# Forming the weight sums of three down projections by accumulating transfers in device memory instead of on VectorE

## The chip, the cores and the metric

The kernel runs on one core of a Trainium2 chip. The metric is the device time of one execution in microseconds (us); lower is better. The kernel before takes 1844.03 us, the median of three runs (1843.58 to 1845.5). Engines are named as in the profile: PE is TensorE's matmul, PEld its weight load, DVE is VectorE, ACT is ScalarE, POOL is GpSimd, SP is SyncE, which here only issues transfers.

## The reference

One sequence of 512 tokens of width 1024 goes through a first block (depth 1) and a second block (depth 2). Each of the three layers ends in a feed-forward part whose last matmul is the down projection; these are what the change is about:

```
# first block                                # second block, for l in 0, 1
a  = square(relu(h2 @ w_up))                 z  = dwconv(h2 @ w_up[l]); zg, zv = split(z)
ff = a @ w_down        # (512,4096)(4096,1024)  x = x + (silu(zg) * zv) @ w_down[l]  # (512,2816)(2816,1024)
```

Ahead of them stand pooling and stick-breaking attention (first block), and latent attention with a 31-tap depthwise convolution (each layer of the second). All is in float32.

## The kernel before

All large matmuls are done as three float32r matmuls (high times high, low times high, high times low). So each weight chunk (128 by 512, 256 KB) is loaded by SP into a raw slot, rounded by ACT to its high part (`w_hi`), and DVE takes the rest (`w_lo`, counted by the semaphore `w_split`). PE then uses it and counts `w_used`.

The three down projections are multiplied in Winograd's form of a 2 by 2 block product, with seven products in place of eight. For that, each pair q of inner blocks (16 pairs in the first block, 11 in each layer of the second; 38 in all) has its four weight blocks w11, w12, w21, w22 combined into four sums t1 to t4. In the kernel before these sums are made ahead of time, while the layer's earlier weights are still being multiplied:

- SP loads the four blocks of a pair into four buffers in on-chip memory (L889 for the first block, L996 for the second).
- DVE makes the four sums in place, one instruction each, in `factor_sum`, and counts each in `t_made`. They are strewn among DVE's other work by the tables `FIRST_SUMS` and `SUM_ORDER`.
- SP stores the four sums to a tensor in device memory, `factor_sums1` or `factor_sums` (L895, L1003).

In the down projection (L920 for the first block, L1026 for the second) SP loads the chunks in the order `DOWN_ORDER`: first the products with w11, t3, t2, t1 of all pairs (`PASS1`), then those with w21, t4, w22 (`PASS2`). A sum is thus read back from device memory like any other weight. Before chunk 4 of a down projection SP waits until the last stores have landed.

Each engine runs its own program in order. POOL's program is short: constants, the windowed sums of the pooling (`pool_group`, L1110 to L1120), then in each layer of the second block the diagonal matrices for the convolution (`diagonals`, L1145) and a sum of squares (L1077). PE's convolution matmuls (L3571) read those diagonals.

## Time and profile before

| | |
|---|---|
| median of 3 runs | 1844.03 us |
| the profiled execution's own time | 1845.35 us |
| its span (first to last instruction) | 1843.5 us |
| mean granted TensorE clock | 0.998 of full |
| PE / PEld / DVE / ACT / POOL busy | 99% / 80% / 77% / 55% / 4% |
| moved by DMA | 281.24 MB, 153 GB/s on the mean |

The profile page gives busy time per engine. Matmuls overlap in the pipeline: a 512-column matmul is shown as 0.39 us long, but one starts each 0.227 us. So PE's busy share says only that it hardly idles. Idle time is shown in front of the instruction that ends it, with the engine or transfer that it waited for.

### The profile page before, as it was taken

The numbers are of one execution on the slowest core, as the hardware profiler recorded it, in microseconds if no ns is written. First come the engines' busy times: TensorE is split into PE (matmuls) and PEld (weight loads), VectorE is DVE, ScalarE is ACT, GpSimd is POOL, SyncE is SP. The second block draws the span as 40 slices with busy tenths as digits, with TensorE's granted clock in tenths as the row PEclk, the third lists the DMA queues.
The fourth block names the chain that finished last, engine by engine and source line by source line (L and its number), as shares of the span: only waits on it lengthen the run. The fifth ranks groups of instructions, "written<-read, shape, count | busy, mean of one in ns | idle before, by whom it ended". The sixth has DMA issues, their size and how long they took to land.

```text
span 1843.5 us, 26684 instructions
## 1 busy us (share of the span) xinstructions
PE 1816.2 (99%) x9225; PEld 1482.6 (80%) x9225; DVE 1416.6 (77%) x2566; ACT 1021.9 (55%) x1911; POOL 75.2 (4%) x110
## 2 busy tenths in 40 slices
PE   8999999999999999999999999999999999999998
PEld 7888878788788878577888888998757878888786
DVE  5887776876687877786578888986877578778978
ACT  6777664544476664566444435664556553344666
POOL 1111100000000000100200000000010020000000
PEclk9999999999999999999999999999999999999999
DMA  4222236398766624511446756643541235676664
GB/s 149 78 78 72 80 123 209 111 318 299 246 220 186 195 78 107 106 46 36 118 154 209 235 190 211 212 156 87 120 84 41 68 108 190 195 246 201 207 195 137
DMA packets 229459, 281.24 MB, mean 153 GB/s; under 512 B 55250, under 2 KB 130016, under 8 KB 229344
## 3 DMA queue, kind: packets, MB, share of 16 engines
q1 hardware_dynamic: 229240, 279.76, 48.7%
q8 instruction: 62, 1.02, 0.2%
q14 instruction: 53, 0.43, 0.1%
q10 hardware_dynamic: 104, 0.03, 0.0%
HBM read 228.98 MB, written 41.94 MB: 147 GB/s over the span
## 4 chain that ended last, share of the span: by engine, by line
PE 87%; DVE 8%; ACT 3%; issue 1%; DMA 1%; SPq 0%; ACTq 0%; DVEq 0%
PE bank_b L3064 14%; PE bank_b L3066 14%; PE bank_b L3065 14%; PE bank_a L3064 11%; PE bank_a L3066 11%; PE bank_a L3065 11%; PE bank_b L3571 2%; PE bank_b L3675 2%; DVE w_lo L1920 2%; DVE arena L1920 1%; PE bank_a L3656 1%; DVE arena L1923 1%; PE bank_a L3091 1%; PE bank_a L3094 1%; PE bank_a L3097 1%
## 5 line engine op out<-in xcount | busy, mean ns | idle before, releaser
L1920 DVE TENSOR_TENSOR w_lo<-w_raw,w_hi 128x512 fp32r<-128x512 f32 (+1 forms) x599 | 391.9, 672 | 198.5 <-ACT w_hi L1577 127.9
L3064 PE MATMUL bank_b<-h_hi,w_hi 128*128 128x512 f32 (+1 forms) x952 | 372.9, 392 | 1.0 <-DVE w_lo L1920 0.6
L3066 PE MATMUL bank_b<-h_hi,w_lo 128*128 128x512 f32 (+1 forms) x952 | 369.3, 388 | 0.0
L3065 PE MATMUL bank_b<-h_lo,w_hi 128*128 128x512 f32 (+1 forms) x952 | 369.0, 388 | 0.0
L1577 ACT ACTIVATE w_hi<-w_raw 128x512 fp32r<-128x512 f32 (+3 forms) x308 | 176.4, 589 | 244.7 <-PE bank_b L3066 93.4
L3064 PEld LDWEIGHTS bank_b<-h_hi,w_hi 128*128 128x128 f32 x952 | 178.8, 188 | 41.1 <-DVE w_lo L1920 2.9
L3065 PEld LDWEIGHTS bank_b<-h_lo,w_hi 128*128 128x128 f32 x952 | 178.8, 188 | 36.9 <-issue 1.4
L3066 PEld LDWEIGHTS bank_b<-h_hi,w_lo 128*128 128x128 f32 x952 | 178.7, 188 | 36.9
L3064 PE MATMUL bank_a<-h_hi,w_hi 128*128 128x512 f32 x513 | 201.1, 392 | 0.4
L3066 PE MATMUL bank_a<-h_hi,w_lo 128*128 128x512 f32 x513 | 199.6, 389 | 0.0
L3065 PE MATMUL bank_a<-h_lo,w_hi 128*128 128x512 f32 x513 | 199.6, 389 | 0.0
L1166 ACT ACTIVATE w_hi<-w_raw 128x512 fp32r<-128x512 f32 x161 | 97.3, 625 | 114.3 <-PE bank_b L3066 55.3
L1920 DVE TENSOR_TENSOR split<-arena,split 128x512 fp32r<-128x512 f32 (+4 forms) x220 | 123.0, 581 | 40.0 <-ACT split L1512 22.6
L1923 DVE SCALAR_TENSOR_TENSOR arena<-arena,cols_all 128x512 f32<-128x512 f32 x176 | 126.3, 745 | 0.0
L3064 PEld LDWEIGHTS bank_a<-h_hi,w_hi 128*128 128x128 f32 x513 | 96.3, 188 | 23.4 <-DVE w_lo L1920 3.3
L3066 PEld LDWEIGHTS bank_a<-h_hi,w_lo 128*128 128x128 f32 x513 | 96.3, 188 | 20.2
L3065 PEld LDWEIGHTS bank_a<-h_lo,w_hi 128*128 128x128 f32 x513 | 96.3, 188 | 20.1 <-issue 0.5
L1501 ACT ACTIVATE w_hi<-w_raw 128x512 fp32r<-128x512 f32 x130 | 78.3, 625 | 42.0 <-PE bank_b L3066 31.1
L1512 ACT ACTIVATE split<-arena 128x512 fp32r<-128x512 f32 (+1 forms) x114 | 62.5, 554 | 46.7 <-PE bank_b L3066 27.7
L1920 DVE TENSOR_TENSOR split_f<-split_f 128x512 f32<-128x512 f32 x102 | 69.7, 685 | 8.1 <-DMA split_f<-in_w_down_dram 8.0
L1823 ACT ACTIVATE arena<-arena,cols_all 128x512 f32<-128x512 f32 x80 | 58.8, 806 | 30.3 <-DVE arena L1920 30.3
L3064 PE MATMUL bank_b<-split,w_hi 128*128 128x512 f32 (+1 forms) x196 | 72.7, 371 | 0.0
(456 smaller groups left out, 3554.1 us busy)
## 6 DMA issues: line engine op xcount, KB each, us to landing
w_raw<-in_w_up_dram SPq DMA_DIRECT2D x240, 256.0 KB, 4.0
split_f<-in_w_down_dram SPq DMA_DIRECT2D x110, 256.0 KB, 4.7
factor_sums<-split_f SPq DMA_DIRECT2D x104, 256.0 KB, 4.2
w_raw<-factor_sums SPq DMA_DIRECT2D x79, 256.0 KB, 3.5
w_raw<-in_w_down_dram SPq DMA_DIRECT2D x51, 256.0 KB, 3.0
ssum<-in_w_down_dram SPq DMA_DIRECT2D x34, 256.0 KB, 3.1
arena<-arena SPq DMA_DIRECT2D x32, 268.0 KB, 4.1
w_raw<-in_w_in_dram SPq DMA_DIRECT2D x64, 128.0 KB, 2.4
```

The lines of the kernel that those rows point to most:

```text
L1166: nc.scalar.activation(w_hi[:, s, :], w_raw[:, s, :], ACT.Copy).then_inc(w_round, 1)
L1501: nc.scalar.activation(ring_hi(l, n), raw_of(l, n), ACT.Copy).then_inc(w_round, 1)
L1512: nc.scalar.activation(as_hi[:, u % 4, 0:unit_cols(l, u)], unit(l, u), ACT.Copy).then_inc(as_round, 1)
L1577: nc.scalar.activation(w_hi[:, s, 0:c], w_raw[:, s, 0:c], ACT.Copy).then_inc(w_round, 1)
L1823: nc.scalar.activation(cz[:, j, :], zp[:, j, 1:1 + S], ACT.Identity, scale=cols_all[:, l, bass.ds(tile + (L_FTAP + 2 * F2T), 1)], bias=col ...
L1920: return nc.vector.tensor_tensor(out_, a, b, op)
L1923: return nc.vector.scalar_tensor_tensor(out=out_, in0=a, scalar=s, in1=b, op0=op0, op1=op1)
L3064: nc.tensor.matmul(out_, a_hi, b_hi, start=start, stop=False, skip_group_check=loose)
L3065: nc.tensor.matmul(out_, a_hi, b_lo, start=False, stop=False, skip_group_check=loose)
L3066: return nc.tensor.matmul(out_, a_lo, b_hi, start=False, stop=stop, skip_group_check=loose)
L3571: last = nc.tensor.matmul(conv_banks[j][rows, :], diag[:, r, rows], stacks[j % 2][:, c, SHIFTS * r:SHIFTS * r + S], start=r == 0, stop=r = ...
L3675: last = nc.tensor.matmul(bank_b[rows, i % 2, c], vv[:, kb, i, rows], pts[(2 * j + hd) % len(pts)][:, kb * P:kb * P + P], start=kb == 0, s ...
```

## The change

DVE's `factor_sum`, its buffers and SP's loads and stores for it are gone. After `pool_group(3)` POOL issues transfers from device memory to device memory: plain copies of the blocks into the tensors of sums, and then transfers that add their source onto the destination (`accum_op`). As only additions are used, the definitions of the sums change sign here and there, and the sums of activations and the final updates on DVE take the opposite sign in exchange (the same number of instructions, `ALU.add` and `ALU.subtract` swapped). `move` issues one transfer, `moved` lets POOL wait until all so far have landed, and `t_made` now counts landed transfers. SP waits for `t_made` before each load of a sum in the down projection. The number of transfers that carry the sums is the same (304 of 256 KB).

```diff
+MOVES_FIRST, MOVES_LAST, MOVES = 6, 2, 8
...
+        def sums_made(l, kind, q):
+
+            if l >= 0:
+                return 16 * (MOVES * DPS[FIRST] + MOVES * (l * DP + q + 1))
+            if kind == "t4":
+                return 16 * (MOVES_FIRST * DPS[FIRST] + 4 * MOVES_LAST * (q // 4 + 1))
+            return 16 * MOVES_FIRST * (q + 1)
...
-            def first_moves(n):
-
-                for q in FIRST_STORES.get(n, ()):
-                    store_first(q)
-                for q, part in FIRST_LOADS.get(n, ()):
-                    sem, landed = sums_moved(FIRST, q, 0)
-                    sp_.wait_ge(sem, landed)
-                    sp_.dma_start(sum_buf(FIRST, q)[part], down_v[:, 2 * q + part // 2, part % 2, :]).then_inc(sem, 16)
-
-            def store_first(q):
-
-                sp_.wait_ge(t_made, 4 * q + 4)
-                for n, kind in enumerate(("t2", "t1", "t4", "t3")):
-                    sp_.dma_start(factor_sums1[q, KINDS.index(kind)], sum_buf(FIRST, q)[n]).then_inc(sums_moved(FIRST, q, 0)[0], 16)
-
...
-                if n == SLOTS:
-                    for m in range(N_DOWN, N_DOWN + SLOTS + 4):
-                        first_moves(m)
-                    store_first(DPS[FIRST] - 1)
-                    for m in range(DPS[FIRST] - FIRST_BUFS, DPS[FIRST]):
-                        sp_.wait_ge(*sums_moved(FIRST, m, 2))
                 if n < SLOTS:
                     sp_.wait_ge(w_split, N_DOWN + n - SLOTS + 1)
                 elif n >= RING:
                     sp_.wait_ge(w_split, N_DOWN + n - RING + 1)
                 if kind in KINDS:
+                    sp_.wait_ge(t_made, sums_made(FIRST, kind, q))
                     src = factor_sums1[q, KINDS.index(kind)]
...
+            moves = 0
+
+            def move(into, src, op=None):
+
+                nonlocal moves
+                moves += 1
+                if op is None:
+                    pool.dma_start(into, src).then_inc(t_made, 16)
+                else:
+                    pool.dma_start(into, src, accum_op=op, max_dma_last_dim=4 * S).then_inc(t_made, 16)
+
+            def moved():
+
+                pool.wait_ge(t_made, 16 * moves)
+
+            def blocks(src, q):
+
+                return [[src[:, 2 * q + two, half, :] for half in range(2)] for two in range(2)]
+
+            for q in range(DPS[FIRST]):
+                (w11, w12), (w21, w22) = blocks(down_v, q)
+                t1, t2, t3, t4 = (factor_sums1[q, n] for n in range(4))
+                move(t1, w11)
+                move(t3, w22)
+                move(t2, w11)
+                moved()
+                move(t1, w12, ALU.add)
+                move(t3, w12, ALU.add)
+                moved()
+                move(t2, t3, ALU.add)
+                moved()
+            for q0 in range(0, DPS[FIRST], 4):
+                for q in range(q0, q0 + 4):
+                    move(factor_sums1[q, 3], blocks(down_v, q)[1][0])
+                moved()
+                for q in range(q0, q0 + 4):
+                    move(factor_sums1[q, 3], factor_sums1[q, 1], ALU.add)
+                moved()
+
+            def layer_sums(l, pairs):
+
+                for q in pairs:
+                    (w11, w12), (w21, w22) = blocks(down2_v[l], q)
+                    t1, t2, t3, t4 = (factor_sums[l, q, n] for n in range(4))
+                    move(t1, w11)
+                    move(t3, w22)
+                    move(t2, w11)
+                    move(t4, w21)
+                    moved()
+                    move(t1, w12, ALU.add)
+                    move(t3, w12, ALU.add)
+                    moved()
+                    move(t2, t3, ALU.add)
+                    moved()
+                    move(t4, t2, ALU.add)
+                    moved()
+
             for l in range(DEPTH2):
+                if l == 0:
+                    layer_sums(0, range(5))
                 was = before(l)
                 sq0, added0 = was["sq_ready"], was["sq_added"]
                 pool.wait_ge(sq_added, added0 + KT - 1)
...
+                if l == 0:
+                    layer_sums(0, range(5, DP))
+                    layer_sums(1, range(DP))
...
-            for q in (DPS[FIRST] - 3, DPS[FIRST] - 2):
-                act.wait_ge(*sums_moved(FIRST, q, 2))
...
-            def factor_sum(l, q, turn):
-
-                w11, w12, w21, w22 = sum_buf(l, q)
-                if turn == 0:
-                    dve.wait_ge(*sums_moved(l, q, 1))
-                else:
-                    dve.wait_ge(t_made, 4 * PAIRS_BEFORE[l] + 4 * q + turn)
-                into, a, b, op = ((w22, w22, w12, ALU.subtract), (w12, w12, w11, ALU.subtract), (w11, w22, w11, ALU.add),
-                                  (w21, w21, w11, ALU.subtract))[turn]
-                tt(into, a, b, op).then_inc(t_made, 1)
 
             def act_sums(l, q, made):
 
                 x11, x21, x22 = arena[:, 2 * q, 0:HS], arena[:, 2 * q, HS:S], arena[:, 2 * q + 1, HS:S]
                 dve.wait_ge(a_ready, made)
-                tt(s13(l, q)[:, 0:HS], x21, x22, ALU.add).then_inc(s_made, 1)
+                tt(s13(l, q)[:, 0:HS], x21, x22, ALU.subtract).then_inc(s_made, 1)
                 tt(s13(l, q)[:, HS:S], x11, x21, ALU.subtract).then_inc(s_made, 1)
...
-                tt(arena[:, 2 * q, 0:HS], arena[:, 2 * q + 1, 0:HS], arena[:, 2 * q, HS:S], ALU.subtract).then_inc(s4_made, 1)
-
...
```

Where the work stands in the engines' programs. POOL of the kernel before, from the end of the last pooling group to its end (L1145 are the diagonals of a layer, L1077 its sum of squares):

```order
L1120 TENSOR_TENSOR arena<-sq,arena 128x496
L1145 TENSOR_TENSOR arena<-cols_all,lanes 128x128 x26
L1077 TENSOR_TENSOR ssum<-sq 128x512
L1077 TENSOR_TENSOR ssum<-ssum,sq 128x512 x6
L1145 TENSOR_TENSOR arena<-cols_all,lanes 128x128 x26
L1077 TENSOR_TENSOR ssum<-sq 128x512
L1077 TENSOR_TENSOR ssum<-ssum,sq 128x512 x6
L348 UNCONDITIONAL_BRANCH
```

POOL of the change around the diagonals of the second block's first layer (its lines are numbered anew: L1057 is a copying transfer, L1059 an adding one, L1122 the diagonals, L995 the sum of squares):

```order
L1057 DMA factor_sums<-in_w_down_dram 128x512 x4
L1059 DMA factor_sums<-in_w_down_dram 128x512 x2
L1059 DMA factor_sums<-factor_sums 128x512 x2
L1122 TENSOR_TENSOR arena<-cols_all,lanes 128x128 x26
L995 TENSOR_TENSOR ssum<-sq 128x512
L995 TENSOR_TENSOR ssum<-ssum,sq 128x512 x6
L1057 DMA factor_sums<-in_w_down_dram 128x512 x4
L1059 DMA factor_sums<-in_w_down_dram 128x512 x2
```

What was one run of tensor instructions now has 168 transfers ahead of the first layer's diagonals (128 for the first block, 40 for 5 pairs of layer 0) and 136 ahead of the second layer's (6 pairs of layer 0, 11 of layer 1), each diagonal behind all of them.

SP of the kernel before, at the start of the first down projection (L920), with the semaphores waited for in brackets:

```order
L920 DMA w_raw<-factor_sums 128x512 [waits w_split]
L895 DMA factor_sums<-split_f 128x512 [waits t_made]
L895 DMA factor_sums<-split_f 128x512 x3
L895 DMA factor_sums<-ssum 128x512 [waits t_made]
L895 DMA factor_sums<-var 128x512
L895 DMA factor_sums<-rs 128x512
L895 DMA factor_sums<-rstd 128x512
L920 DMA ssum<-factor_sums 128x512 [waits raw_moved2,raw_moved1,raw_moved0]
L920 DMA var<-factor_sums 128x512
L920 DMA rs<-factor_sums 128x512
L920 DMA rstd<-factor_sums 128x512
```

SP of the change further on in the same down projection (now L856):

```order
L856 DMA w_raw<-factor_sums 128x512 [waits t_made,w_split]
L856 DMA ssum<-in_w_down_dram 128x512 [waits w_split]
L856 DMA var<-in_w_down_dram 128x512 [waits w_split]
L856 DMA rs<-factor_sums 128x512 [waits t_made,w_split]
L856 DMA rstd<-in_w_down_dram 128x512 [waits w_split]
```

The stores between SP's loads are gone, and the loads of sums wait for POOL's transfers by `t_made`.

## Rows read from the trace of the kernel before

**Rows 1.** The page: busy time, then PE, granted clock and DMA in 40 slices.

```profile
PE 1816.2 (99%) x9225; PEld 1482.6 (80%) x9225; DVE 1416.6 (77%) x2566; ACT 1021.9 (55%) x1911; POOL 75.2 (4%) x110
...
PE   8999999999999999999999999999999999999998
...
PEclk9999999999999999999999999999999999999999
DMA  4222236398766624511446756643541235676664
```

**Rows 2.** Waits of PE: all the run, then of 1700 to 1750 alone (us, times, longest).

```profile
PE bank_a L3171 <- DMA arena<-in_x_dram: 4.6, 1, 4.6
PE bank_a L3064 <- ACT arena L1743: 4.4, 6, 1.3
PE bank_a L3064 <- DVE split L1920: 3.3, 4, 2.2
...
PE bank_b L3064 <- DVE w_lo L1920: 0.6, 3, 0.2
...
PE bank_a L3064 <- DVE split L1920: 0.6, 2, 0.3
```

**Rows 3.** Stretches: length, then busy time (instructions) of each engine, clock, DMA share, GB/s.

```profile
348.00:485.00 137.00, 137.00 (x604) 113.09 (x603) 96.95 (x170) 59.94 (x107) 0.00 (x0) 1.00 0.84 283
912.00:1127.00 215.00, 214.75 (x942) 175.87 (x941) 172.24 (x287) 88.76 (x139) 0.33 (x1) 1.00 0.62 199
1250.00:1338.00 88.00, 87.52 (x381) 71.04 (x380) 63.70 (x116) 41.73 (x75) 3.10 (x6) 1.00 0.43 103
1500.00:1706.00 206.00, 205.85 (x905) 168.69 (x904) 165.32 (x277) 85.54 (x134) 0.00 (x0) 1.00 0.61 199
```

**Rows 4.** One form of DVE's weight sums: busy us, mean ns, then idle before.

```profile
L1920 DVE TENSOR_TENSOR split_f<-split_f 128x512 f32<-128x512 f32 x102 | 69.7, 685 | 8.1 <-DMA split_f<-in_w_down_dram 8.0
```

**Rows 5.** Start of the first down projection, in time: start us, us, instruction; PE, then ACT.

```profile
504.44 0.57 PE L3064 MATMUL bank_a<-w_hi,split 128*128 128x512 f32 x1 [2.20 <-DVE split L1920]
504.81 0.63 PE L3065 MATMUL bank_a<-w_lo,split 128*128 128x512 f32 x1
...
508.16 0.40 PE L3064 MATMUL bank_a<-w_hi,split 128*128 128x512 f32 x1
508.40 0.40 PE L3065 MATMUL bank_a<-w_lo,split 128*128 128x512 f32 x1
...
502.34 0.63 ACT L1501 ACTIVATE w_hi<-w_raw 128x512 fp32r<-128x512 f32 x1 [2.09 <-PE bank_b L3066]
502.87 0.61 ACT L1512 ACTIVATE split<-arena 128x512 fp32r<-128x512 f32 x1
```

**Rows 6.** POOL in time, from its last pooling instruction; idle before in brackets.

```profile
202.47 1.25 POOL L1120 TENSOR_TENSOR arena<-sq,arena 128x496 f32<-128x496 f32 x1 [4.01 <-DVE w_lo L1920]
685.30 3.04 POOL L1145 TENSOR_TENSOR arena<-cols_all,lanes 128x128 f32<-128x128 f32 x6 [481.57 <-DVE ssum L1920]
...
906.15 6.17 POOL L1077 TENSOR_TENSOR ssum<-ssum,sq 128x512 f32<-128x512 f32 x4 [3.77 <-ACT sq L1180]
1266.24 3.10 POOL L1145 TENSOR_TENSOR arena<-cols_all,lanes 128x128 f32<-128x128 f32 x6 [353.91 <-DVE ssum L1920]
```

**Rows 7.** PE's first convolution matmuls of either layer, in time.

```profile
754.92 5.36 PE L3571 MATMUL bank_a<-arena 128*32 128x512 f32 x48
1338.65 2.35 PE L3571 MATMUL bank_a<-arena 128*32 128x512 f32 x20
```

**Rows 8.** SP's loads in time: t3 of pair 0, t3 of pair 15, t4 of pairs 0 and 1; layer 0.

```profile
488.76 0.33 SPq L920 DMA_DIRECT2D w_raw<-factor_sums  x1
570.37 0.32 SPq L920 DMA_DIRECT2D var<-factor_sums  x1
577.15 1.69 SPq L920 DMA_DIRECT2D w_raw<-factor_sums  x2
1132.24 0.43 SPq L1026 DMA_DIRECT2D var<-factor_sums  x1
```

**Rows 9.** Transfers of `split_f`: issue time in ns (min/median/max), then issue to landing in us.

```profile
L895 SPq DMA_DIRECT2D factor_sums<-split_f x48: 429/462/1111, 299.2 to 495.3; - x48
DMA to landing us min/median/max: 2.5/4.4/7.3
```

**Rows 10.** Transfers of `factor_sums` (stores and loads back): issue to landing in us.

```profile
DMA to landing us min/median/max: 2.0/3.8/6.4
```

More of the change, by code:

```diff
@@ L16 @@
 from contextlib import ExitStack
-from itertools import islice
 import concourse.bass as bass
@@ L509, in two_blocks @@
         first_raw = (ssum[:, :], var[:, :], arena[:, 31, :], split_f[:, 20, :])
-        sum_bufs = [[split_f[:, n, :] for n in range(4)], [split_f[:, n, :] for n in range(4, 8)], [sq[:, n, :] for n in range(4)],
-                    [split_f[:, 8, :], split_f[:, 9, :], rs0[:, :], rs1[:, :]]]
         factor_sums = nc.dram_tensor("factor_sums", (DEPTH2, DP, 4, P, S), F32)
@@ L519, in two_blocks @@
         raw1 = (ssum[:, :], var[:, :], rs1[:, :], rstd[:, 0, :])
-        bufs1 = [[split_f[:, n, :] for n in range(4)], [split_f[:, n, :] for n in range(4, 8)], list(raw1)]
-        early1 = [split_f[:, n, :] for n in range(17, 21)]
         factor_sums1 = nc.dram_tensor("factor_sums1", (F1T // 2, 4, P, S), F32)
@@ L1022, in _ @@
                     if kind in KINDS:
+                        sp_.wait_ge(t_made, sums_made(l, kind, q))
                         src = factor_sums[l, q, KINDS.index(kind)]
@@ L1974, in fourth_sum, with update @@
                 dve.wait_ge(as_ready, units_before(l) + 2 * q + 1)
-                tt(arena[:, 2 * q, 0:HS], arena[:, 2 * q + 1, 0:HS], arena[:, 2 * q, HS:S], ALU.subtract).then_inc(s4_made, 1)
-            def update(name, t, after, into, src, made, count):
+                tt(arena[:, 2 * q, 0:HS], arena[:, 2 * q + 1, 0:HS], arena[:, 2 * q, HS:S], ALU.add).then_inc(s4_made, 1)
+            def update(name, t, after, into, src, made, count, op=ALU.add):
                 dve.wait_ge(made, count)
@@ L2934, in ffn_tiles @@
                                 ALU.mult, ALU.add).then_inc(done, 1)
-                            for q, turn in islice(sums, 1):
-                                factor_sum(l, q, turn)
                         split(tap // 2)
```

84 lines of the change are left out of this document (13 added, 71 removed).

## The prediction

> **What bounds the kernel now.** I read the page's busy times first. PE is busy 1816.2 of 1843.5 us and no other engine is near it: DVE has 77%, POOL 4% [rows 1]. The 40 slices show the same from end to end, at full clock. As busy matmuls overlap, I then asked the waits of PE, for only what PE waits for can be won by unburdening another engine. PE waits for DVE 3.3 us for its splits and 0.6 us for `w_lo`, in all [rows 2]. Then the stretches in which DVE makes the weight sums: 348 to 485 (first block) and 912 to 1127 and 1500 to 1706 (second). PE has 604, 942 and 905 matmuls in 137, 215 and 206 us, one each 0.227 to 0.228 us, and idles for 0.00, 0.25 and 0.15 us. In 1250 to 1338, where DVE makes no weight sums, the pace is 381 in 88 us, 0.231 us each, no faster [rows 3]. So the sums lie wholly beside the matmuls, and they don't slow their pace either.
>
> **What is removed.** 38 pairs by 4 sums are 152 DVE instructions (102 of them in the form of [rows 4]) by 0.685 us, 104 us of DVE's 1416.6. All of it lies beside a PE that hardly idles, so I cost it at nothing but the waits. Of PE's 3.3 us for DVE's splits, 2.2 us is one gap at 502.2 to 504.4, the start of the first down projection [rows 5], and 0.6 us lies at 1700 to 1750, the start of the last one [rows 2].
>
> The change takes ACT's wait for the stores of pairs 13 and 14 out of just this place, so it has to be asked whether the 2.2 us goes. ACT rounds four weight chunks and then the units of the activations. The fourth chunk is rounded at 502.34, after a wait of 2.09 us that ended with a PE matmul (its slot had to come free), and the first unit follows at 502.87, at once [rows 5]. So the removed wait was over, and what is late is PE's own last matmul of the up projection followed by ACT, DVE and PE in turn. ACT's order is the same in the change: the gap stays. The slow stretch behind it stays too: nine matmuls start 0.43 us apart instead of 0.23, which is 1.8 us (the first starts at 504.44, the tenth at 508.16, so 3.72 us for nine). SP's loads of the down projection no longer wait behind eight stores, but PE has no wait for a transfer there [rows 2], so that is worth nothing. The gain I take is 0.5 us, most of the 0.6 us at 1700 to 1750.
>
> **What is added.** 304 transfers on POOL, each 256 KB, device memory to device memory, in waves: POOL issues a few, waits until all have landed, issues the next. The chain is serial, and what stands behind it in POOL's order is waited for by PE. The trace has no transfer issued by POOL, none from device memory to device memory and none that adds. So I set up the deadlines exactly and bound the price.
>
> Deadlines. POOL is free at 202.47 + 1.25 = 203.7 and after that does nothing until the diagonals at 685.3 [rows 6]. But these 685.3 are no deadline: PE first reads diagonals at 754.9 [rows 7]. By then POOL has to make 76 waves (first block 16 x 3 and 4 x 2, layer 0 5 x 4), 551 us for them. Within these, t1 to t3 of pair 15 are wanted at 570.4 and t4 of pairs 0 to 3 at 577.2 [rows 8]. After the sum of squares at 906.15 + 6.17 = 912.3 [rows 6], POOL has 17 pairs of 4 waves ahead of the second layer's diagonals, which PE reads at 1338.65 [rows 7]: 426.3 us, 25.1 us a pair, 6.3 us a wave. That is the tightest. Layer 0's own down projection begins at 1132 [rows 8], by when its 6 pairs are long made, if a pair takes under 36 us.
>
> Price. Let s be the time to issue one more transfer, c the time from issue to landing of a copy, a that of an adding one. The nearest rows are SP's transfers of the same size to and from `split_f` under the same load: s = 0.46 us, c = 4.4 us median, with 2.5 and 7.3 us as the ends [rows 9]. `factor_sums` alone lands in 2.0 to 6.4 us, median 3.8 [rows 10]. Low end: 2.0 us for either kind. High end, if read and write came strictly one after the other: c = 3.8 + 3.9, say 7.7, and a = 11.6 with the second operand's read. I take c = 4.4, since reading and writing stream through together, and for a the middle between the median and the longest landing, 5.9 us (an estimate from 4.4 and 7.3), as an add reads twice what it writes. With s = 0.45:
> - a pair of the first block, t1 to t3: (2s + c) + (s + a) + a = 17.6 us; 16 pairs end at 203.7 + 281 = 485, and 570 is wanted.
> - four t4: (3s + c) + (3s + a) = 13.0 us; the first four end at 498 (577 wanted), all at 537.
> - a pair of the second block: (3s + c) + (s + a) + a + a = 23.9 us; 5 pairs end at 656, before POOL's old 685.
> - 17 pairs: 406 us, from 912 to 1319, where 1338.65 is wanted. It fits with 20 us to spare, or 0.4 us in a.
>
> The diagonals begin some 50 us later than now in the second layer (1319 for 1266), which their cover, PE's work until 1338, hides. Waits added on SP: each load of a sum waits for `t_made`, and all later weight loads are behind it; they are satisfied before SP comes there in all three projections. Traffic: the sums' transfers keep their number, but device memory now sees 304 writes where it saw 152, and 456 reads where it saw 152 (a copy reads once, each of the 152 adds twice), 40 and 80 MB more, spread over 204 to 1320. In 348 to 485 DMA is at 0.84 busy today without one wait of PE [rows 3], so I cost the spreading at nothing.
>
> A rule speaks against my price of the add. The Trainium skill, Collectives: The Full Stack, section on the bandwidth ceiling, says that a reduce runs at half the rate of a copy because its two source reads share one ring. Taken on the whole landing time, that makes a = 8.8 us, the second rival below. Taken on the moving part alone it is little. No row here shows it.
>
> **Sum.** 1843.5 - 0.5 + 0 = 1843.0 us of span, with the 1.85 us outside it 1844.85 for a profiled execution that took 1845.35. That execution lies 1.3 us above the median of the runs, so the median comes to 1843.5 us.
>
> **Rivals.**
> - Faster: 1840. Freed of 104 us, DVE and ACT meet PE in time at 502, and the 2.2 us gap and the 1.8 us of slow matmuls behind it go. Against it: ACT there waited for PE, not for DVE [rows 5].
> - Small loss, 1848 to 1855. More read and write traffic in stretches where SP's loads are urgent, or POOL's issuing work slowing DVE, makes PE wait now and then; ten waits of 0.5 to 1 us would do. Against it: the 0.84 busy stretch.
> - Slower, the chain misses its last deadline. The mechanism: POOL reaches the second layer's diagonals late, and PE stands at its first convolution matmul. It decides from a = 6.3 us on, and then costs 51 us for each us in a. With a = 7.3, the longest landing in [rows 9], a pair takes 28.1 us, 17 take 478, and PE waits 51 us: 1895. The first chain, 524 us, ends at 727 and still fits.
> - Far slower, a = 8.8: a pair 32.6 us, 17 take 554, 128 us late; the first chain 23.4 x 16 + 15.9 x 4 + 32.6 x 5 = 601 us, 49 us late at 754.9 (7 of them already at pair 15). Together 177: 2021. At the high end, a pair of 44.3 us makes 327 us late, and the first chain 274: 2445.
>
> The Trainium skill, DMA: Bandwidth & Descriptors, section on the anatomy of one DMA issued by GpSimd, gives 2.0 us plus bytes over 436 GB/s, 2.6 us here as an estimate; by that alone a pair would take some 12 us and no deadline would be near. The loads and stores of the trace take 3.8 to 4.4 us on the median, so the rows decide.
>
> **How the numbers follow.** A measurement of this kernel tells from no change what is over about 0.2%, 3.7 us. Chances: no change as forecast 0.48 (1841 to 1847); faster 0.10; small loss 0.10; the last deadline missed 0.20 (1855 to 1935); far slower 0.12. So slower has 0.42. The range takes in faster, the small loss and the greater part of the missed deadline: 1840 to 1910. Its upper end leaves out about 0.18.
>
> **What would show it.** Right: DVE's busy time down by about 104 us with PE's matmul count and pace unchanged; the wait of 2.2 us at 502 still there; POOL's diagonals of the second layer starting between 1290 and 1338; no wait of PE for L1145's successor, L1122. A landing time of the adding transfers of 5.9 us confirms the price, below 6.3 the verdict. Wrong: PE idle before the convolution matmuls with POOL named as the releaser; SP waiting for `t_made` in the first down projection, which would show that 22.9 us a pair is passed; or the gap at 502 gone.

## The result and the profile after

The change made the kernel slower by 0.6%: 1856.95 us, the median of six runs (1851.69 to 1857.69), for 1845.36 of six runs of the kernel before beside them (1843.58 to 1847.42). The medians differ by 11.6 us; the ratio is 1.0059 [1.0049, 1.0069], which is 9 to 13 us. The forecast was no change. The profiled execution took 1856.91 us, its span is 1854.8 us, and 11.3 us more than the span before is what has to be explained.

The page of the changed kernel, the lines that answer to [rows 1], and of its DMA and chain sections the lines needed below (q0 is the queue of POOL's transfers: packets, MB, share of the time of the 16 DMA engines):

```profile
PE 1816.5 (98%) x9225; PEld 1484.2 (80%) x9225; DVE 1329.3 (72%) x2414; ACT 1022.9 (55%) x1911; POOL 281.3 (15%) x414
...
POOL 1111222222222211100222211112220020000000
...
DMA  4222577677799966411477778887841123333554
...
q0 software_dynamic: 34048, 79.71, 21.3%
...
HBM read 268.83 MB, written 81.79 MB: 189 GB/s over the span
...
PE 68%; DMA 20%; DVE 4%; issue 3%; POOL 2%; ACT 2%; SPq 0%; DVEq 0%; ACTq 0%; POOLq 0%
```

PE does the same 9225 matmuls in the same busy time. DVE is relieved of 152 instructions and 87 us of busy time (1416.6 to 1329.3). The 104 us forecast were 152 by 0.685, and the durations of DVE's instructions do add up to 104 us less (1464.7 for 1569.1); busy time counts a stretch in which two overlap only once, so it falls by 0.57 us for each. The chain that ended last now runs to 20% through DMA and to 2% through POOL: the chain of waves of transfers has become a part of the critical path.

What PE waits for, in all, as in [rows 2] (us, times, longest):

```profile
PE bank_a L3534 <- POOL arena L1122: 5.3, 1, 5.3
...
PE bank_b L3027 <- issue: 4.0, 2, 3.9
PE bank_a L3027 <- DVE split L1898: 2.8, 2, 2.2
PE bank_a L3066 <- DVE ssum L1898: 2.6, 2, 2.1
```

Of the last one the kernel before has this:

```profile
PE bank_a L3103 <- DVE ssum L1920: 1.0, 2, 0.5
```

Two waits are new, and the last has grown: its longer one, now 2.1 us for 0.5, ends at 1313.3. The first is the one that the prediction named as the sign of a missed deadline: a convolution matmul with POOL's diagonals (L1122) as the releaser. PE in time at the four places in question (start us, us, instruction, idle before), for [rows 5] and [rows 7]:

```profile
504.56 0.47 PE L3027 MATMUL bank_a<-w_hi,split 128*128 128x512 f32 x1 [2.20 <-DVE split L1898]
...
753.51 5.36 PE L3534 MATMUL bank_a<-arena 128*32 128x512 f32 x48
...
1336.03 0.47 PE L3027 MATMUL bank_b<-split,w_hi 128*128 128x512 f32 x1 [3.86 <-issue]
...
1349.59 7.49 PE L3534 MATMUL bank_a<-arena 128*32 128x512 f32 x48 [5.31 <-POOL arena L1122]
```

The gap at 502 is there unchanged with its 2.20 us, and the first layer's convolution starts at 753.5, 1.4 us earlier than before. The second layer's starts at 1349.6, where it was 1338.65: 10.9 us of the 11.3 have arisen by then.

POOL in time, for [rows 6]: the first layer's diagonals, then the first pair of the second chain (L1057 a plain copy, L1059 an adding transfer), then its end.

```profile
711.64 2.64 POOL L1122 TENSOR_TENSOR arena<-cols_all,lanes 128x128 f32<-128x128 f32 x6 [3.40 <-DMA factor_sums<-factor_sums]
...
911.01 2.14 POOL L1057 DMA_DIRECT2D factor_sums<-in_w_down_dram  x4
920.59 1.72 POOL L1059 DMA_DIRECT2D factor_sums<-in_w_down_dram  x2 [7.44 <-DMA factor_sums<-in_w_down_dram]
928.21 0.80 POOL L1059 DMA_DIRECT2D factor_sums<-factor_sums  x1 [5.89 <-DMA factor_sums<-in_w_down_dram]
932.50 0.81 POOL L1059 DMA_DIRECT2D factor_sums<-factor_sums  x1 [3.49 <-DMA factor_sums<-factor_sums]
936.97 2.12 POOL L1057 DMA_DIRECT2D factor_sums<-in_w_down_dram  x4 [3.65 <-DMA factor_sums<-factor_sums]
...
1344.97 0.81 POOL L1059 DMA_DIRECT2D factor_sums<-factor_sums  x1 [3.51 <-DMA factor_sums<-factor_sums]
1349.05 3.54 POOL L1122 TENSOR_TENSOR arena<-cols_all,lanes 128x128 f32<-128x128 f32 x7 [3.28 <-DMA factor_sums<-factor_sums]
```

The first pair's waves take 9.58, 7.62, 4.29 and 4.47 us, 25.96 in all. The 17 pairs run from 911.0 to 1349.05, 438 us, 25.8 us a pair on the mean, where 25.1 was the break-even and 23.9 the forecast. They are not alike: from start to start the first eight (911 to 1105) take 24.3 us each, the next five (to 1252) 29.4, the last four 24.3. PE's matmul starts 0.54 us after the diagonals begin.

How long POOL takes to issue a transfer, and how long one takes to land, for [rows 9] and [rows 10] (ns min/median/max, first and last start; then us):

```profile
L1057 POOL DMA_DIRECT2D factor_sums<-in_w_down_dram x152: 523/552/771, 204.2 to 1327.3; - x152
...
DMA to landing us min/median/max: 2.7/4.7/8.2
```

```profile
L1059 POOL DMA_DIRECT2D factor_sums<-in_w_down_dram x76: 839/871/1172, 209.8 to 1334.5; - x76
L1059 POOL DMA_DIRECT2D factor_sums<-factor_sums x76: 802/807/1771, 217.3 to 1345.0; - x76
...
DMA to landing us min/median/max: 3.9/5.2/11.4
```

The other new wait, 3.9 us before 1336.03, does not name POOL. The profile has only "issue" for it, so the link is read from the times: PE starts 0.1 us after ACT's three squares out of `bank_b` (L1160, 1334.38 to 1335.93), the bank that PE writes next. In ACT's order they stand behind the rounding of a small weight chunk, and that waited for its load. Here ACT at this chunk in the change (the first fence) and in the kernel before (the second):

```profile
1334.06 0.42 ACT L1555 ACTIVATE w_hi<-w_raw 128x256 fp32r<-128x256 f32 x1 [5.44 <-DMA w_raw<-in_w_uq_dram]
```

```profile
1329.69 0.42 ACT L1577 ACTIVATE w_hi<-w_raw 128x256 fp32r<-128x256 f32 x1 [0.87 <-DMA w_raw<-in_w_uq_dram]
```

ACT gets that chunk 4.4 us later, while POOL's last waves are under way. SP did not issue its loads later: they start at 1324.0 here and at 1324.2 before. They land later. Issue to landing (us, min/median/max) of the ten loads of `w_uq` issued up to 1330.3, in the change and in the kernel before:

```profile
DMA to landing us min/median/max: 3.7/4.4/6.4
```

```profile
DMA to landing us min/median/max: 1.7/1.9/3.9
```

The stretches around it (length, busy time of each engine, granted clock, DMA share, GB/s), the first two as in [rows 3]:

```profile
348.00:485.00 137.00, 137.00 (x605) 113.06 (x604) 68.89 (x122) 59.73 (x107) 31.61 (x47) 1.00 0.74 187
912.00:1127.00 215.00, 214.78 (x944) 176.74 (x944) 149.76 (x248) 91.02 (x142) 47.20 (x70) 1.00 0.77 188
1100.00:1250.00 150.00, 150.00 (x1105) 142.99 (x1104) 124.96 (x216) 93.85 (x167) 28.01 (x41) 1.00 0.84 232
...
1336.00:1340.00 4.00, 3.97 (x9) 2.55 (x10) 2.98 (x7) 2.29 (x5) 0.00 (x0) 0.61 1.07 168
1348.00:1352.00 4.00, 2.41 (x12) 0.68 (x16) 2.78 (x5) 3.91 (x9) 2.95 (x6) 0.50 0.11 22
```

Behind each of the two idle times the granted clock is lower: 0.50 in 1348 to 1352, which is the lower level of 1.2 GHz, and 0.61 on the mean in 1336 to 1340, where nine matmuls fill 4 us. The wait of 2.1 us before 1313.3, the idle time of 3.9 us and the slow stretch behind it make PE ready for the convolution only at 1344.3 (1349.59 less 5.31). Counted from the start of layer 0's down projection, PE gets there 7.5 us sooner where nothing disturbs it (198.05 us in the table below, for 205.6 here). That by itself is not paid for: the diagonals came at 1349.05 anyway. So POOL's lateness alone suffices for the 11 us, and what the late loads would cost without it is for an experiment.

### The profile page after: what moved, and what is told of

The parts are those of the page before. It is cut to its first block, busy times and chain, and to the rows that moved or that the text cites. A ratio compares the mean times of both kernels' runs of the same rounds, so it can differ in the third digit from the quotient of the medians.

```text
span 1854.8 us, 26670 instructions
## 1 busy us (share of the span) xinstructions
PE 1816.5 (98%) x9225; PEld 1484.2 (80%) x9225; DVE 1329.3 (72%) x2414; ACT 1022.9 (55%) x1911; POOL 281.3 (15%) x414
## 3 DMA queue, kind: packets, MB, share of 16 engines
q0 software_dynamic: 34048, 79.71, 21.3%
HBM read 268.83 MB, written 81.79 MB: 189 GB/s over the span
## 4 chain that ended last, share of the span: by engine, by line
PE 68%; DMA 20%; DVE 4%; issue 3%; POOL 2%; ACT 2%; SPq 0%; DVEq 0%; ACTq 0%; POOLq 0%
PE bank_b L3027 11%; DMA factor_sums<-in_w_down_dram 11%; PE bank_b L3029 11%; PE bank_b L3028 11%; DMA factor_sums<-factor_sums 9%; PE bank_a L3027 8%; PE bank_a L3029 8%; PE bank_a L3028 8%; PE bank_b L3534 2%; PE bank_b L3638 2%; POOL factor_sums L1057 1%; PE bank_a L3619 1%; DVE w_lo L1898 1%; PE bank_a L3054 1%; PE bank_a L3057 1%
## 5 line engine op out<-in xcount | busy, mean ns | idle before, releaser
L1901 DVE SCALAR_TENSOR_TENSOR arena<-arena,cols_all 128x512 f32<-128x512 f32 x176 | 120.5, 744 | 0.0
L1059 POOL DMA_DIRECT2D factor_sums<-factor_sums x76 | 61.9, 911 | 330.2 <-DMA factor_sums<-in_w_down_dram 230.7
L1057 POOL DMA_DIRECT2D factor_sums<-in_w_down_dram x152 | 81.2, 544 | 194.5 <-DMA factor_sums<-factor_sums 183.2
L1059 POOL DMA_DIRECT2D factor_sums<-in_w_down_dram x76 | 64.7, 998 | 206.6 <-DMA factor_sums<-in_w_down_dram 202.5
```

Of the source, the lines that this page charges most:

```text
L1057: pool.dma_start(into, src).then_inc(t_made, 16)
L1059: pool.dma_start(into, src, accum_op=op, max_dma_last_dim=4 * S).then_inc(t_made, 16)
L1901: return nc.vector.scalar_tensor_tensor(out=out_, in0=a, scalar=s, in1=b, op0=op0, op1=op1)
```

## Experiments

The theory after the result: the second chain ends some 11 us too late, because a pair costs 25.8 us on the mean. Its rivals: that the transfers beside the small loads cost the time by themselves, and that the end of the chain is of no matter. Whether DVE's relief is worth nothing was open too. Kernels that were timed stood beside 15 to 31 runs of the kernel before, with medians of 1844.42 to 1845.13 us.

**One pair more ahead of the first layer's diagonals, one fewer behind.**

```diff
-                    layer_sums(0, range(5))
+                    layer_sums(0, range(6))
...
-                    layer_sums(0, range(5, DP))
+                    layer_sums(0, range(6, DP))
```

> The change, with six pairs of layer 0 summed ahead of that layer's diagonals in place of five, so that 16 pairs in place of 17 stand ahead of the second layer's diagonals. Theory (the loss is POOL's lateness at the second layer's diagonals): at 25.8 us a pair the second chain ends near 1323, before PE's first convolution matmul at 1338, the first chain ends near 736 and PE wants its diagonals at 754, so nothing is late: 1844 to 1846 us, 11 to 12 below the change. Rival (the loss is spread, from the larger traffic and POOL's issuing): at most one third of it goes, 1852 or more.

Measured: 1846.4 us (1844.67 to 1850.05, 11 runs), ratio 1.0015 [1.0006, 1.0024]. POOL at the second layer's diagonals, then PE at the convolution:

```profile
1318.70 3.40 POOL L1122 TENSOR_TENSOR arena<-cols_all,lanes 128x128 f32<-128x128 f32 x6 [3.60 <-DMA factor_sums<-factor_sums]
```

```profile
1340.31 5.36 PE L3534 MATMUL bank_a<-arena 128*32 128x512 f32 x48
```

The diagonals of the chain of 16 pairs start 21.6 us before PE wants them, and PE does not wait. A change that only moves one pair takes back 10.6 us. It doesn't tell the two theories apart, though: with one pair fewer the chain also ends before the small loads of 1324 to 1340. And 1.3 us are left between the medians (1 to 4 by the interval). In the trace the wait for `ssum`, here before 1315.2, is 1.6 us for 0.5, beside the chain's last waves.

**Six pairs of layer 1 only after that layer's sum of squares.** They are not needed before its own down projection.

```diff
-                    layer_sums(1, range(DP))
+                    layer_sums(1, range(5))
+                else:
+                    layer_sums(1, range(5, DP))
```

> The change, with pairs 5 to 10 of layer 1 summed after that layer's sum of squares (from about 1490 on), so that 11 pairs stand ahead of the second layer's diagonals and the chain ends near 1195. Theory: 1844 to 1846 us, the same as with six pairs, though the transfers are now away from the whole stretch 1195 to 1490. Rival (traffic beside the second layer's small weight loads also costs where nothing is late): this kernel is faster than the one with six pairs by 2 us or more. The late pairs end near 1650, and the down projection wants pair 5 after 1715.

Measured: 1844.95 us (1843.39 to 1847.52, 11 runs), ratio 1.0005 [0.9996, 1.0014], no difference from before. POOL reaches the diagonals about when the kernel before did (1266.24), and the wait for `ssum` is back at 0.5 us:

```profile
1268.26 1.96 POOL L1122 TENSOR_TENSOR arena<-cols_all,lanes 128x128 f32<-128x128 f32 x3 [74.70 <-DVE ssum L1900]
```

**Transfers beside the small loads, with the chain in time.** The kernel with six pairs, and after its diagonals six spare transfers of the same sizes and kinds into a tensor that nobody reads.

```diff
...
                 diagonals(0)
+                if l == 1:
+                    (w11, w12), (w21, w22) = blocks(down2_v[l], 0)
+                    for n, src in enumerate((w11, w22, w11, w21)):
+                        move(spare[n], src)
+                    moved()
+                    for n in range(2):
+                        move(spare[n], w12, ALU.add)
+                    moved()
...
```

> As the kernel with six pairs, and after the first seven diagonals of the second layer POOL moves six transfers (four copies, two adding) into a tensor that nobody reads, from about 1323 to 1340, beside the small weight loads of that layer. If contention alone makes those loads late, PE idles near 1332 for about 4 us, as it did with the change, and the time is 4 to 6 us above that with six pairs. If only lateness counts, it is the same as with six pairs within 1 us.

Measured: 1850.03 us (1848.31 to 1851.02, 9 runs), ratio 1.0028 [1.0018, 1.0038]; 3.6 us more than with six pairs alone, near the 4 to 6 us expected of contention. POOL at the spare transfers, and PE at its one long wait before the convolution:

```profile
1320.69 4.29 POOL L1123 TENSOR_TENSOR arena<-cols_all,lanes 128x128 f32<-128x128 f32 x6 [3.78 <-DMA factor_sums<-factor_sums]
1324.93 2.15 POOL L1058 DMA_DIRECT2D spare<-in_w_down_dram  x4
```

```profile
1316.45 2.07 PE L3075 MATMUL bank_a<-ssum,ones 128*128 128x512 f32 x2 [3.70 <-DVE ssum L1907]
```

But this wait ends 8.5 us before the first spare transfer is issued. It is the wait for `ssum` again (1.6 us with six pairs), beside the last waves of the chain itself, with the clock at 0.50 in 1316 to 1320 behind it. PE has lost nothing more when it comes to the convolution: in the table below it is there 4.9 us later than with six pairs, all of it by 1326.4, and behind it up to the next up projection 0.4 us are added. So the spare transfers did not cost this execution its time, and what makes the medians differ by 3.6 us is open. (The spare tensor also stands ahead of `factor_sums` in device memory; whether that matters wasn't tried.)

That transfers in flight hold up the small loads is shown by comparing the traces. The wait for `ssum` near 1313 is 0.5 us in the kernel before, in the one with sums of one column below, and in all six versions whose transfers are over by then. It is 1.6, 2.1, 2.5 and 3.7 us in the four where the chain still runs: six pairs, the change, four pairs, and this one. The small loads of 1324 to 1330 land after 4.4 us on the median beside the change's last waves, after 2.0 us with six pairs. In these executions such waits, with the slow clock behind them, make PE 1.1 us (six pairs), 6.0 us (this one) and 7.5 us (the change) later at the convolution than PE is undisturbed; in the change that lay inside POOL's lateness. The proof that lateness by itself costs time is the next experiment.

**One more pair behind than in the change.** Four pairs of layer 0 ahead of its diagonals, 18 behind; the diff is that of the first experiment with 4 for 6.

> The change with four pairs of layer 0 ahead of the first layer's diagonals and 18 pairs ahead of the second's. By lateness alone each pair more costs its whole 25.8 us: 1878 to 1884 us, with PE waiting some 31 us for L1122 near 1344. If the loss came from traffic or from the number of transfers, which are the same, the time stays at 1857.

Measured: 1878.55 us (1871.84 to 1880.68, 4 runs), ratio 1.019 [1.0174, 1.0206], 21.6 us above the change on the median. Number and kind of the transfers are those of the change. In the profiled execution, at 1871.84 the fastest of the four, PE stands at the convolution (31 us were expected):

```profile
1364.79 1.94 PE L3534 MATMUL bank_a<-arena 128*32 128x512 f32 x8 [23.11 <-POOL arena L1122]
```

**Seven pairs ahead of the first layer's diagonals.** This pushes the first chain to its own deadline.

> The change with seven pairs of layer 0 ahead of the first layer's diagonals. The second chain (15 pairs) ends near 1300, in time; the first ends near 761, 7 to 8 us after PE wants its diagonals at 753.5. Theory of deadlines: PE waits for L1122 near 754 to 761 and no longer at 1344, and the time is 7 to 9 us above that with six pairs, 1853 to 1856. Rival (the loss sits in the second layer's stretch alone, not at whichever deadline is missed): 1844 to 1847.

Measured: 1850.99 us (1848.24 to 1856.11, 4 runs), ratio 1.0044 [1.0027, 1.0062], less than expected. POOL and PE of the profiled execution (1848.66 us):

```profile
758.47 2.16 POOL L1122 TENSOR_TENSOR arena<-cols_all,lanes 128x128 f32<-128x128 f32 x3 [3.35 <-DMA factor_sums<-factor_sums]
```

```profile
751.75 0.47 PE L3027 MATMUL bank_b<-split,w_hi 128*128 128x512 f32 x1 [2.81 <-issue]
...
759.93 5.36 PE L3534 MATMUL bank_a<-arena 128*32 128x512 f32 x48
```

Here the diagonals came 1.5 us before their matmul, and the wait that was expected is not there: PE had already lost its time at 751.75 and at 730.1, where its wait for `ssum` is 2.35 us for 0.5. These are the same two kinds of wait as at 1313 and 1336 in the change, again beside the chain's waves. PE would not have fared better without them, since the diagonals at 758.47 are later than the 754.9 of before. So with 5 pairs the second deadline is missed, with 7 the first, and of the splits tried only 6 fits both.

**The same chain without adding.** Every adding transfer is a plain copy; the sums are not made.

```diff
-                    pool.dma_start(into, src, accum_op=op, max_dma_last_dim=4 * S).then_inc(t_made, 16)
+                    pool.dma_start(into, src).then_inc(t_made, 16)
```

> The change with each adding transfer made a plain copy (the sums are left out: the tensors hold single blocks). Number, order and size are the same. If adding costs only in POOL's issue (0.87 us against 0.55), a pair takes 24.5 us; if it also costs in the engines, since an add reads two operands, a pair takes 20 to 22 us, and the second chain ends at 1250 to 1285 in place of 1349.

One run, 1843.32 us. Issue times, POOL's queue on the page, and the second layer's diagonals:

```profile
L1059 POOL DMA_DIRECT2D factor_sums<-in_w_down_dram x76: 523/523/535, 210.8 to 1258.9; - x76
L1059 POOL DMA_DIRECT2D factor_sums<-factor_sums x76: 486/497/502, 215.2 to 1266.5; - x76
```

```profile
q0 software_dynamic: 20672, 79.71, 13.7%
```

```profile
1270.30 2.65 POOL L1122 TENSOR_TENSOR arena<-cols_all,lanes 128x128 f32<-128x128 f32 x6 [3.32 <-DMA factor_sums<-factor_sums]
```

The chain is 78.8 us shorter (1270.30 for 1349.05), 4.6 us a pair or 1.16 us for each of the 68 waves, of which 51 add. A pair takes 21.1 us on the mean, in the range expected if an add also costs in the engines. From start to start of the waves between 911 and 1100 (means over 7 to 18 waves):

| wave of | copies (this kernel) | as in the change |
|---|---|---|
| 1 transfer | 3.34 us | add: 4.66 us |
| 2 transfers | 5.27 us | adds: 6.83 us |
| 4 copies | 7.83 us | 7.96 us |

An add costs some 1.3 us more than a copy in a wave of one, 1.6 us in a wave of two. Of that 0.3 us is POOL's issuing (0.81 for 0.50 us). The DMA engines have more to do as well: for the same 79.71 MB the packets of POOL's queue take 21.3% of the engines' time with adds and 13.7% without. If the 152 copies cost half of 13.7% in either kernel, an add takes some 2.1 times the engine time of a copy (an estimate), though its wave lasts only 1.4 times as long. The bytes read from device memory don't tell the two apart: the page has 268.83 MB read for both kernels.

**Two pairs a wave.** The transfers of pairs 2n and 2n+1 are issued together, so that there are half as many waits.

```diff
-                for q in pairs:
...
+                for n in range(0, len(pairs), 2):
+                    two = [(blocks(down2_v[l], q), [factor_sums[l, q, m] for m in range(4)]) for q in pairs[n:n + 2]]
+                    for ((w11, w12), (w21, w22)), (t1, t2, t3, t4) in two:
+                        move(t1, w11)
+                        move(t3, w22)
+                        move(t2, w11)
+                        move(t4, w21)
+                    moved()
...
```

> The change with two pairs in each wave in place of one (t4 of the first block stays by fours), the order else the same. If a wave's price is mostly the wait for landing, a group of two pairs takes some 29 to 33 us in place of 51.6: the first chain ends near 600, the second near 1200, nothing is late, and the time is 1843 to 1847. If the price is bytes through the DMA engines, two pairs take 45 us or more and the second chain ends after 1290. Denser bursts could cost PE more beside its loads: above 1847.

Measured: 1843.73 us (1842.56 to 1844.88, 11 runs), ratio 0.9996 [0.9987, 1.0005]. POOL in one group of two pairs, and at the diagonals:

```profile
946.72 4.18 POOL L1058 DMA_DIRECT2D factor_sums<-in_w_down_dram  x8 [5.82 <-DMA factor_sums<-factor_sums]
958.00 3.36 POOL L1060 DMA_DIRECT2D factor_sums<-in_w_down_dram  x4 [7.10 <-DMA factor_sums<-in_w_down_dram]
968.74 1.64 POOL L1060 DMA_DIRECT2D factor_sums<-factor_sums  x2 [7.37 <-DMA factor_sums<-in_w_down_dram]
974.49 1.64 POOL L1060 DMA_DIRECT2D factor_sums<-factor_sums  x2 [4.11 <-DMA factor_sums<-factor_sums]
980.15 4.18 POOL L1058 DMA_DIRECT2D factor_sums<-in_w_down_dram  x8 [4.02 <-DMA factor_sums<-factor_sums]
...
1265.51 3.04 POOL L1128 TENSOR_TENSOR arena<-cols_all,lanes 128x128 f32<-128x128 f32 x6 [26.13 <-DVE ssum L1904]
```

Two pairs take 33.4 us here (946.72 to 980.15), the shortest of eight such groups; they take 33.4 to 44.0, on the mean 37.9 us or 18.9 a pair, more than the 29 to 33 expected and less than the 45 of the rival. The chain is done 26 us before DVE releases the diagonals, and the loss is gone.

**The kernel before, with DVE's weight sums cut to one column.** The instructions and all waits stay; the sums are not made.

```diff
-                tt(into, a, b, op).then_inc(t_made, 1)
+                tt(into[:, 0:1], a[:, 0:1], b[:, 0:1], op).then_inc(t_made, 1)
```

> The kernel before, its 152 weight sums on DVE cut to one column each (so the sums are left out but for a column), everything else in place. DVE has some 95 us less to do. Theory (these sums lie wholly beside the matmuls): 1844 to 1846 us, no difference. Rival (DVE's load does hold PE back somewhere): faster by 3 us or more.

Measured: 1842.19 us (1841.16 to 1842.74, 11 runs), ratio 0.9986 [0.9977, 0.9995], 2.9 us less. That is a small gain whose interval leaves out no change: DVE's sums did cost something. The stretch behind the gap at 502, in the kernel before and in this one:

```profile
500.00:512.00 12.00, 9.80 (x36) 7.66 (x36) 6.60 (x11) 9.91 (x20) 0.00 (x0) 0.86 0.84 271
```

```profile
500.00:512.00 12.00, 9.80 (x43) 7.80 (x42) 6.29 (x10) 9.20 (x18) 0.00 (x0) 1.00 0.75 255
```

Without the fall of the clock to 0.86, seven more matmuls start in these 12 us. But the profiled execution of the change also has full clock there, and others have not, with the same gap of 2.2 us before it, so I can't tie it to the edit.

**Transfers put where loads are light.** Two versions. The first keeps single pairs: 5, 4 and 2 pairs of layer 0, 7 and 4 of layer 1, the middle groups ahead of the sums of squares:

```diff
+                if l == 0:
+                    layer_sums(0, range(5, 9))
+                else:
+                    layer_sums(1, range(7, DP))
                 pool.wait_ge(stat_ready, was["stat_ready"] + 4)
                 add_squares(KT,
...
```

> The change, its transfers placed where PE's weight loads are light: 5 pairs of layer 0 ahead of the diagonals as in the change, 4 pairs of layer 0 after the diagonals (from 782, done near 885), 2 pairs of layer 0 and 7 of layer 1 after the sum of squares (911 to some 1140), the last 4 of layer 1 after its diagonals (1366 to some 1470). Nothing is late by the measured 25.8 us a pair. Theory (lateness plus what the transfers' traffic takes beside the loads): 1843 to 1845, at or a little below the kernel with the late pairs after the sum of squares (1844.95). Rival (placement does not matter once nothing is late): equal to that kernel within 0.5 us.

Measured: 1844.08 us (1842.25 to 1844.83, 11 runs), ratio 0.9996 [0.9987, 1.0005].

The second takes two pairs a wave as above, all 11 pairs of layer 0 ahead of its diagonals, and of layer 1 six pairs ahead of layer 0's sum of squares and five ahead of its own, so that no transfer of POOL lies beside an up projection of the second block:

```diff
-                    layer_sums(0, range(5))
+                    layer_sums(0, range(DP))
...
+                layer_sums(1, range(6, DP) if l else range(6))
                 pool.wait_ge(stat_ready, was["stat_ready"] + 4)
...
```

> Two pairs in each wave, and all transfers kept out of the two stretches in which PE works through the up projections of the second block: all 11 pairs of layer 0 ahead of its diagonals (done near 711, wanted at 753.5), 6 pairs of layer 1 after layer 0's diagonals (782 to 887, the sum of squares is at 897), the last 5 after layer 1's diagonals (1366 to 1471, then the sum of squares at 1481). Theory (what DVE's freedom brings, 2.9 us by the kernel with thin sums, is taken back by transfers beside the up projections): 1841.5 to 1843, below the kernel before by 2 to 3 us and below the one with two pairs a wave by 1. Rival (the take-back is elsewhere): 1843.5 to 1844.5, as with two pairs a wave.

Measured: 1844.64 us (1843.5 to 1849.16, 11 runs), ratio 1.0004 [0.9995, 1.0013]. The expected gain did not come.

**Where the last microseconds are.** Distances between PE's first matmuls of successive parts, from the traces of the profiled executions (us):

| kernel | first down projection to first convolution | to layer 0's up projection | to its down projection | to second convolution | to layer 1's up projection | to its down projection | to the end |
|---|---|---|---|---|---|---|---|
| before | 250.48 | 165.64 | 219.82 | 198.27 | 165.33 | 219.95 | 110.78 |
| sums of one column | 248.88 | 165.54 | 218.95 | 198.05 | 165.52 | 218.93 | 109.95 |
| the change | 248.95 | 165.81 | 219.40 | 210.87 | 167.5 | 218.93 | 109.95 |
| six pairs | 249.67 | 165.82 | 220.23 | 199.15 | 166.02 | 218.93 | 109.95 |
| six pairs and spare transfers | 250.13 | 165.77 | 219.60 | 204.08 | 166.40 | 218.97 | 109.95 |
| late pairs | 250.69 | 165.82 | 219.99 | 198.05 | 165.74 | 220.60 | 109.95 |
| two pairs a wave | 248.99 | 165.46 | 219.91 | 198.03 | 165.74 | 218.98 | 109.94 |
| no transfer beside up projections | 250.78 | 165.85 | 218.98 | 198.05 | 165.82 | 218.93 | 109.95 |

The change against the kernel before, from left to right: -1.5, +0.2, -0.4, +12.6, +2.2, -1.0, -0.8, in sum +11.3. The +2.2 stand behind the wait for POOL, where the clock is at 0.50. The first column goes by the clock at 502: the traces with 250.5 to 250.8 us have 0.86 in 500 to 512, the others 1.00. DVE's relief gives 0.8 us in the last down projection in every version. In an up projection it gives about 1.0 us (218.9 for 219.9), unless POOL's transfers lie beside it: these take between 0.5 and 1.7 us of it back. These are profiles of one execution each, and I show their agreement, not an interval. The last version wins both up projections and has the fall of the clock at 502, which makes its first column 1.9 us longer than with sums of one column; why it came here is open.

## Why the prediction was wrong

**The deadlines were right.** POOL's start at 203.7, the two deadlines at 754.9 and 1338.65 and their order of tightness hold: the chain misses the second only, and where it is given one pair fewer it fits (six pairs), one more and it is 15 to 22 us later (four pairs). The mechanism of the loss is that of the third rival, with its price at the mild end: that rival decided from a pair of 25.1 us on, and a pair took 25.8. Its condition in a, 6.3 us or more, was not met on the mean: a single add took 4.66 us up to 1100, less than my 5.9, and 6.06 between 1100 and 1250. My sign that a landing below 6.3 us confirms the verdict was no sign: the median is 5.2, and the deadline was missed.

**The step that failed is the price of a wave: 23.9 us a pair for all 17, wherever they stand.** Together they cost 438 us for 406, which takes the 20 us to spare and 11 more. By stretches the miss is not spread evenly. The twelve pairs outside 1105 to 1252 cost 24.3 us each, 4 us too much in all; at that price 17 pairs end at 1323 and fit. The five pairs inside cost 29.4 each, 27 us too much. There I costed the waves beside layer 0's down projection like all others. In 1100 to 1250 the DMA engines are busy to 0.84 with 232 GB/s, where the kernel before moved 188 GB/s. In the kernel without adds the five pairs of this stretch are slower too, 24.3 us for 19.7 before it. That the fuller engines are the cause fits all this; no experiment isolates it.

**Within the price, s and a were both wrong.** I took s = 0.45 us, SP's issue time, as the cost of each further transfer in a wave, and a landing time for a single one. Four copies were (3s + c) = 5.75 us by that. Measured are 7.96 us, and the series in the kernel without adds, 3.34, 5.27 and 7.83 us for 1, 2 and 4 copies, shows how: a lone copy is cheaper than I took c for (3.34, issue included, for 4.4), but each further one adds 1.3 to 1.9 us. With eight in a wave it is 12.66 us, 1.2 us each. POOL's issue time of 0.55 us is less than half of that. That the transfers of one wave share what moves them would explain the rest; it is not shown. For adds the same: 4.66 us alone, where I had taken 5.9, and 2.2 us for the second.

By terms a pair in the stretch 911 to 1100 costs 7.96 + 6.83 + 2 x 4.66 = 24.1 us, for 23.9 forecast: the errors of the two terms nearly cancel, by luck. Between 1100 and 1250 it is 8.33 + 8.23 + 2 x 6.06 = 28.7, each kind of wave dearer.

**The margin was misread.** I wrote "20 us to spare, or 0.4 us in a". Spread over 68 waves, 20 us are 0.3 us a wave, less than the difference between any two rows that I had taken my prices from ([rows 9], [rows 10]). A forecast with ends of 2.0 and 7.7 us and a break-even so close to the value taken had no ground for 0.48 on the one side.

**First chain.** Forecast to end at 656, it ended at 711.6. The pairs of the first block took 18.2 us for 17.6, 10 us in all; four t4 took 21.4 us for 13.0, 33 us in all; five pairs 26.1 for 23.9, 11 us. The waves with most transfers are the most underpriced, here by the term s. It was hidden by the 43 us of slack that were left.

**DVE's sums at nothing.** Wrong in size: with the sums cut to one column the kernel takes 2.9 us less (1 to 4 by the interval of its ratio), where I had 0.5. In the profiles 2.7 us of it lie in the second block's two up projections and the last down projection. The first block's up projection gains nothing (147.4 us from 357.0 to 504.4, and the same with sums of one column), and 1.6 us of the profiled execution's gain is the clock at 502. PE's pace of 0.227 to 0.228 us a matmul in [rows 3] looked full, but 1 us in 220 is four matmuls of over 900. The list of waits does not show it either. From start to start, some half of it are single delays (a matmul at 1066.6 starts 0.48 us after the one before it, for 0.23), the rest delays of hundredths of a us in some twenty matmuls.

**The gap at 502** stays with 2.20 us, as argued from ACT's wait for PE. The 1.8 us of slow matmuls behind it, which I said would stay too, are a matter of the clock's fall and come and go between executions.

**Traffic at nothing.** Wrong where small loads are urgent: PE's wait for `ssum` near 1313 grows from 0.5 to between 1.6 and 3.7 us, and in the change another of 3.9 us comes at 1336. The 0.84 busy stretch, from which I argued, had no such loads in it. The bytes were wrong too: I forecast 80 MB more read, counting two reads for an add, and the page has 39.85 MB more, just as much as with plain copies.

**The rules.** A single add took 4.66 us and a single copy 3.34 us from wave to wave, so doubling the whole landing (8.8 us) is not borne out. The rule of the Trainium skill, Collectives: The Full Stack, section on the bandwidth ceiling, is that two source reads on one ring halve the rate; the trace agrees with it for the DMA engines' time alone (2.1 times, by the estimate above). The estimate of 2.6 us from the Trainium skill, DMA: Bandwidth & Descriptors, section on the anatomy of one DMA, lies below the 2.7 us that was the shortest landing and far below the median of 4.7.

## What to carry to other kernels

When work goes to a serial chain of waves with a deadline, measure or bound the wave, not the transfer: what a further transfer in a wave costs (here 1.2 to 2.2 us for 256 KB) is not its issue time, and waves beside heavy loads cost a fifth more (29.4 us a pair for 24.3). Price each stretch of the chain by what runs beside it. Compare the slack per wave with the spread of the durations that the price was taken from; if it is smaller, the forecast is open, whatever the middle says. If the chain is too long, merge waves of independent items (25.8 to 18.9 us a pair here) or move one item past the deadline before doubting the idea; but with the engine that was relieved off the critical path, all of this only gets back to the time before.

## What the runs showed of the hardware

- Adding transfers issued by GpSimd work from device memory to device memory. For 256 KB a wave of one takes 4.66 us for 3.34 of a copy, of which 0.3 us is the longer issue (0.81 for 0.50 us). POOL's queue takes 21.3% of the DMA engines' time for 13.7% with copies alone.
- POOL's issue times for copies vary little (523 to 771 ns) with DVE 72% busy; of the adding ones the longest is 1771 ns, the medians 807 and 871.
- Transfers in flight hold up small loads from another queue: ten loads of `w_uq` land after 4.4 us on the median beside the change's waves, for 1.9 us before. PE then idles 3.9 us, and the clock behind it is lower, 0.61 over 4 us in the change, 0.63 at 752 to 756 with seven pairs.
- The sums' 152 more writes show as 39.85 MB more written (81.79 for 41.94 MB). Read are 39.85 MB more (268.83 for 228.98), with adds as with plain copies in their place: the page's figure does not show a second read of an add. Whether it goes uncounted is open.
